# A decoder trunk on one core: the first eight expert picks multiplied one by one beside the retention of the second tile

## The chip, the cores and the metric

The kernel runs on one core of one Trainium2 chip. The metric is the device time of one execution in microseconds (us), and the smaller it is the better. Two numbers are used. The time of a run is what the device reports. The span is what the profiler sees from the first to the last instruction of one profiled execution.

The engines are PE (matmuls; PEld is its weight load), DVE (vector), ACT (activation functions and copies), POOL (here it issues the gathers) and SP (it issues the plain loads). All transfers run on the same 16 DMA engines.

## What is computed

256 tokens, in two tiles of 128, pass two layers of width 1024. Layer 0 mixes the tokens with a sparse attention and a retention, layer 1 with a convolution module. After each mixer stands the expert layer, which takes nearly all the bytes:

```python
def peer_ffn(h, w_q, sub_keys, u, v):
    q = (xf @ w_q).reshape(T, P_HEADS, 2, P_QDIM // 2)
    s1 = jnp.einsum('thd,kd->thk', q[:, :, 0], sub_keys[0])
    s2 = jnp.einsum('thd,kd->thk', q[:, :, 1], sub_keys[1])
    ...
    # top 16 of each, top 16 of their sums: 8 heads x 16 = 128 experts per token, with gates
    def block(args):
        xb, ib, gb = args
        hb = jnp.einsum('td,tkd->tk', xb, u[ib])
        act = jax.nn.gelu(hb, approximate=False) * gb
        return jnp.einsum('tk,tkd->td', act, v[ib])
```

Each token picks 128 experts of 16384, and an expert is one row of u and one of v, 8 KB together in float32. A *pick* below is the k-th expert of all 128 tokens of a tile: one gather of 128 rows of 2048 floats, 1.049 MB. There are 128 picks for each of two tiles in each of two layers, 512 in all.

The retention of layer 0, which the change works beside, is for a tile and a head: q times k, times a decay, times v (and for the second tile also against the first tile's k and v), then a norm over the head, then a product with the swish of a gate. Then attention and retention go through one output projection w_o into the residual, which the expert layer reads.

## The kernel before

The program is written out by hand for five engines, each a queue of instructions in program order, with semaphores between them.

**The ring.** Expert rows are gathered into a ring of 16 slots of 1 MB in SBUF. For pick n, POOL issues the gather (line 498). DVE multiplies the u half with the token's normed input and sums it: one dot per token (line 1042). ACT makes the gelu of the dots of two picks (line 654), times the gates (line 657), and writes it as diagonal matrices of 64 columns (line 663). PE multiplies the v half with the diagonals (line 1491) into accumulators and counts `v_multiplied`. This count frees the slot for a later pick. A round is 16 picks, eight rounds are a tile, and PE, ACT and DVE have other work written in between the picks of a round (the functions `first_beside` and `beside`).

PE multiplies picks in pairs. The matrices are 64 x 64 quadrants of the array: an even pick uses the two quadrants on one diagonal and adds into the PSUM tile `side`, an odd pick those on the other diagonal and adds into `pm`.

**What POOL waits for before it issues pick n.** (a) The slot's last pick was multiplied. `pick_slots` gives each pick its slot and the pick that must be multiplied first. Up to pick 127 this is pick n - 14, because slots 14 and 15 are away, and hold weights, from pick 14 on (`AWAY`). (b) Pick n - 5 has landed (`AHEAD`). (c) The picks of the first round also wait for what lay in the ring before: the input weights w_in and the work tiles of attention and retention. Slots 0 to 2 are free when the second tile's attended values are copied out (`a_ready`), slots 3 to 6 after the projection rq of the second tile, 7 and 8 after its rv, 9 and 10 after its rg (the gate), and 11 and up when the retained values have been copied out (`b_t_ready`). (d) Each round needs its 16 indices, which DVE writes head by head (`heads`, lines 950 to 1028); POOL copies them first (line 481).

**The place of the change** is the end of the second tile's mixer, from 126 to 164 us. PE goes through this order: queries for head 1, attended values, scores, then the projections rq and rv, retention scores, the retained product, the projection rg, the transposes of the result, and after that picks 0, 1, 2, ... ACT and DVE are written in the same order. Among picks 0 to 15 PE also multiplies the queries and scores of heads 2 and 3, with the weight chunks 2 and 3 of wq. SP loads these into slots 14 and 15, and waits for `b_t_ready` of the second tile before it does (`load_kept`, line 387). Once the scores are there, DVE does the selection for both heads in one piece, `heads(0, 1)` at line 1216, after the dots of pick 15 and before the dots of pick 16.

Of the kernel before, what the change touches and what calls it, by code (L numbers as in the profile page):

```python
# [7 lines left out]
D = 1024  # L8
# [29 lines left out]
AHEAD = 5  # L38
BATCH = 4
HALF = P // 2  # L40
COLS = D // 2
# [19 lines left out]
KEPT_IN = {(kind, p, c): r for kind, p, c, r in KEPT}  # L61
AWAY = {10: (PICKS + 6 * RING, 3 * PICKS + RING + 4), 11: (PICKS + 6 * RING, 3 * PICKS + RING + 4), 12: (PICKS, 2 * PICKS + 2 * RING + 12), 13: (PICKS, 2 * PICKS + 2 * RING + 12), 14: (RING - 2, 3 * PICKS + 2 * RING + 8), 15: (RING - 2, 3 * PICKS + 2 * RING + 8)}

# [27 lines left out]
def pick_slots():  # L91

    last, uses, slots = {r: r - RING for r in range(RING)}, {r: 0 for r in range(RING)}, []
    for n in range(4 * PICKS):
        free = [r for r in range(RING) if r not in AWAY or not AWAY[r][0] <= n < AWAY[r][1]]
        r = min(free, key=lambda r: last[r])
        uses[r] += 1
        slots.append((r, uses[r], max(last[r], n - RING)))
        last[r] = n
    return slots  # L100
# [20 lines left out]
def hybrid_decoder_trunk_kernel(nc, x, gains, w_in, kv_norm, uk_t, uv_w, w_o, rot, decay,  # L121
# [9 lines left out]
    with ctx:  # L131
# [314 lines left out]
        def _(pool):  # L446
# [24 lines left out]
            def gathers(p, first, end):  # L471

                layer, t = p // 2, p % 2
                for i in range(first, end):
# [6 lines left out]
                    pool.tensor_copy(idx_now[:, i % 2, :], eidx[:, t, i * RING:(i + 1) * RING]).then_inc(idx_copied, 1)  # L481
                    pool.wait_ge(idx_copied, n0 // RING + 1)
                    for n in range(n0, n0 + RING):
                        r, use, freed = SLOTS[n]
                        if freed >= 0:
                            pool.wait_ge(v_multiplied, RING + freed + 1)
                        if n < RING and r in in_use:
                            if in_use[r]:
                                pool.wait_ge(proj_ps, job_of(*in_use[r]) + 1)
                            else:  # L490
                                pool.wait_ge(b_t_ready, 2)
                        if r in AWAY and n >= AWAY[r][1] and all(SLOTS[m][0] != r for m in range(AWAY[r][1], n)):
                            kind, of, c = [k[:3] for k in KEPT if k[3] == r][-1]
                            pool.wait_ge(*((pw_ps, KD + c + 1) if kind == "w1" else (q_ps, nth_head(of + 1, c // 2, c % 2))))
                        if n >= AHEAD:
                            pool.wait_ge(gathered[SLOTS[n - AHEAD][0]], 16 * SLOTS[n - AHEAD][1])
                        pool.sem_inc(may_gather, 1)
                        pool.indirect_dma_start(ring[:, r, :], None, table[layer],  # L498
                                                bass.IndirectOffsetOnAxis(idx_now[:, i % 2, n - n0:n - n0 + 1], 0)) \
                            .then_inc(gathered[r], 16)  # L500

            pool.wait_ge(a_ready, 2)
            gathers(0, 0, 8)
# [8 lines left out]
        def _(act):  # L512
# [134 lines left out]

            def expert_round(p, i, between=None):

                t = p % 2  # L650
                for first, end in batches(p, i):
                    n0 = p * PICKS + i * RING
                    act.wait_ge(dots_ready, n0 + end)
# [95 lines left out]
            gate_exps(0, 0, (1,))  # L749
            keep_rv(1)  # L750
            root_of_group_norm(1)
            gate_of_retention(1)
            keep_retained(1)
            for i in range(8):
                expert_round(0, i, lambda b: first_beside(i, b))
                if i == 0:
                    gate_exps(0, 1)
            for p in (1, 2, 3):
# [16 lines left out]
        def _(dve):  # L775
# [255 lines left out]

            def expert_round(p, i, between=None):


                t = p % 2

                for r in range(RING):
                    if between:
# [115 lines left out]
            heads(0, 0, (1,))  # L1154
            rotary(1, 0)
            decay_scores(1)
            group_norm(1)
# [56 lines left out]

            expert_round(0, 0)
            heads(0, 1)
# [10 lines left out]
        def _(pe):  # L1227
# [220 lines left out]

            def queries(p, i, b):
# [4 lines left out]
                for j in range(2):  # L1454
                    last = product(ps_q[:, b, j * P:(j + 1) * P], lambda k: w[:, k, j * P:(j + 1) * P], lambda k: of_tile[:, k, :])
                last.then_inc(q_ps, 1)
# [17 lines left out]

            def expert_round(p, i, between=None):

                if p and i == 0:
                    pe.wait_ge(x_ready, (0, 3, 5, 7)[p])
                last_pick = (RING - 1, RING - 3) if (p, i) == LAST else (RING - 2, RING - 1)
                for first, end in batches(p, i):  # L1480
                    for r0 in range(first, end, 2):
                        pair = range(r0, min(r0 + 2, end))
                        pe.wait_ge(diag_ready, p * PICKS + i * RING + pair[-1] + 1)
                        for c in range(2):
                            for r in pair:
                                odd = r % 2 if (p, i) != LAST or r < RING - 1 else 0
                                for half in range(2):
                                    rows = slice(half * HALF, (half + 1) * HALF)
                                    j = (half + odd) % 2
                                    slot = SLOTS[p * PICKS + i * RING + r][0]  # L1490
                                    step = pe.matmul(acc[odd][c][j * HALF:(j + 1) * HALF, :], diag[rows, r % (2 * BATCH), :],  # L1491
                                                     ring[rows, slot, D + c * COLS:D + (c + 1) * COLS],
                                                     start=(i == 0 and r0 == 0), stop=(i == 7 and r == last_pick[odd]))
                                if c and ((p, i) != LAST or r < RING - 1):
                                    step.then_inc(v_multiplied, 1)
                                elif (p, i) == LAST and r == RING - 1:
                                    step.then_inc(last_ps, 1)
                    if between and end % BATCH == 0:
# [96 lines left out]

            for i in range(8):
                expert_round(0, i, lambda b: first_beside(i, b))
# [70 lines left out]
```

## Time and profile before

| | us |
|---|---|
| median of 3 runs | 1567.49 |
| lowest and highest of them | 1563.81, 1574.69 |
| the profiled execution's own time | 1567.84 |
| its span | 1566.1 |
| DMA engines, bytes moved | 611.75 MB, mean 391 GB/s |
| PE, DVE, ACT, POOL busy | 68%, 70%, 33%, 45% of the span |

The page cuts the span into 40 equal slices of 39 us each. Slices 2 to 4 (39 to 157 us) are those in which the DMA engines are less than busy; from slice 5 on they are at 9 tenths or more throughout, at 380 to 422 GB/s up to the last slice. The first gather is issued at 133.4 us.

### The profile page before, as it was taken

The page shows a single profiled execution, that of the slowest core. Times are in us where ns is not written, and L with a number is a line of the kernel's source. Part 1 is how long each engine was busy: PE and PEld are TensorE (multiplying, and loading weights), DVE is VectorE, ACT ScalarE, POOL GpSimd, SP SyncE. Part 2 cuts the span into 40 slices and gives each one's busy share as a digit, 9 for nine tenths or more (in the row PEclk, how much of TensorE's full clock was granted, in tenths as well). Part 3 has the DMA queues.
Part 4 walks back from the last instruction along what each step waited for, and adds up shares of the span by engine and source line. Part 5 has one row for each costly group of instructions (what it writes and reads, how often), then busy time and mean ns, then how long its engine had stood idle before and what let it go on. Part 6 is the DMA issues. An engine that isn't in the chain of part 4 may idle for free.

```text
span 1566.1 us, 20662 instructions
## 1 busy us (share of the span) xinstructions
PE 1057.7 (68%) x6966; PEld 528.1 (34%) x6966; DVE 1101.3 (70%) x2839; ACT 514.7 (33%) x1569; POOL 710.1 (45%) x566
## 2 busy tenths in 40 slices
PE   7999857666674576667746678646767657565655
PEld 7796433332331143323413335312433313111111
DVE  2745567787887678986448889899558878654455
ACT  3222314333232444324313443434243234322223
POOL 0002434344444366675334436575444445454552
PEclk9999978888787788887768889967887879778686
DMA  9147999999999999999999999999999999999996
GB/s 381 55 145 269 372 421 421 420 420 421 418 413 420 416 389 422 416 392 422 421 421 396 406 380 421 420 422 417 420 421 421 420 418 418 410 422 421 421 421 272
DMA packets 85451, 611.75 MB, mean 391 GB/s; under 512 B 9440, under 2 KB 10208, under 8 KB 12640
## 3 DMA queue, kind: packets, MB, share of 16 engines
q0 software_dynamic: 73728, 536.90, 83.2%
q1 hardware_dynamic: 11472, 73.26, 11.6%
q8 instruction: 55, 0.90, 0.2%
q14 instruction: 52, 0.43, 0.1%
q10 hardware_dynamic: 144, 0.26, 0.0%
HBM read 609.34 MB, written 1.05 MB: 390 GB/s over the span
## 4 chain that ended last, share of the span: by engine, by line
DMA 76%; PE 13%; DVE 7%; ACT 2%; issue 1%; DVEq 1%; ACTq 0%; POOL 0%; SPq 0%; POOLq 0%
DMA ring<-experts_dram,idx_now 75%; PE pm L1239 6%; PE side L1491 3%; DVE ring L1042 2%; PE side L1239 2%; DMA ring<-wq_dram 1%; DMA x_tok<-x_dram 0%; PE pm L1380 0%; ACT diag_all L663 0%; PE side L1462 0%; DVE top_i L962 0%; DVE x_tok L1056 0%; DVE onehot L963 0%; DVE top_i L978 0%; DVE conv_buf L1111 0%
## 5 line engine op out<-in xcount | busy, mean ns | idle before, releaser
L498 POOL DMA_INDIRECT ring<-experts_dram,idx_now x512 | 692.5, 1353 | 708.8 <-DMA ring<-experts_dram,idx_now 421.2
L1491 PE MATMUL side<-ring,diag_all 64*64 64x512 f32 x2056 | 650.8, 772 | 476.6 <-ACT diag_all L663 468.0
L1042 DVE SCALAR_TENSOR_TENSOR ring<-ring,h_tok 128x1024 f32<-128x1024 f32 x512 | 611.1, 1224 | 249.5 <-DMA ring<-experts_dram,idx_now 242.7
L1491 PE MATMUL pm<-ring,diag_all 64*64 64x512 f32 x2040 | 647.5, 773 | 0.0
L1491 PEld LDWEIGHTS side<-ring,diag_all 64*64 64x64 f32 x2056 | 153.1, 162 | 897.4 <-ACT diag_all L663 646.6
L654 ACT ACTIVATE ge<-hb 128x2 f32<-128x2 f32 (+1 forms) x257 | 52.4, 204 | 830.7 <-DVE ring L1042 830.3
L663 ACT ACTIVATE diag_all<-ident,act_v 128x64 f32<-128x64 f32 x512 | 150.7, 341 | 21.3 <-issue 0.4
L1491 PEld LDWEIGHTS pm<-ring,diag_all 64*64 64x64 f32 x2040 | 151.7, 162 | 0.0
L657 ACT ACTIVATE act_v<-ge,gates 128x1 f32<-128x1 f32 x512 | 123.5, 288 | 17.7
L1111 DVE SCALAR_TENSOR_TENSOR conv_buf<-conv_buf,chan_sb 128x128 f32<-128x128 f32 x480 | 128.9, 348 | 0.0
L1239 PEld LDWEIGHTS side<-h_t,wbuf 128*128 128x128 f32 x448 | 52.3, 195 | 13.3 <-issue 10.6
L1239 PE MATMUL side<-h_t,wbuf 128*128 128x128 f32 x448 | 54.6, 281 | 2.2 <-ACT h_t L526 2.2
L1239 PE MATMUL pm<-conv_buf,ring 128*128 128x128 f32 x448 | 53.6, 280 | 0.2 <-DVE ring L889 0.2
L654 ACT ACT_TABLE_LOAD x41 | 52.6, 1283 | 1.6
L1239 PEld LDWEIGHTS pm<-conv_buf,ring 128*128 128x128 f32 x448 | 52.3, 194 | 1.4 <-DVE ring L889 0.6
L959 DVE MAX8 top_v<-side 128x8 f32<-128x128 f32 x64 | 15.2, 290 | 49.8 <-PE side L1462 49.6
L481 POOL COPY idx_now<-eidx 128x16 uint32<-128x16 uint32 x32 | 11.0, 345 | 73.1 <-ACT conv_buf L605 72.9
L1042 DVE DVE_READ_ACCUMULATOR ring<-ring,h_tok 128x1 f32 x512 | 42.7, 83 | 0.0
L1239 PEld LDWEIGHTS side<-h_t,ring 128*128 128x128 f32 x320 | 38.6, 201 | 10.5 <-issue 7.3
L1239 PE MATMUL side<-h_t,ring 128*128 128x128 f32 x320 | 40.3, 287 | 2.2 <-DMA ring<-wq_dram 2.2
L1239 PEld LDWEIGHTS pm<-hc_t,wbuf 128*128 128x128 f32 x256 | 32.1, 207 | 10.0 <-issue 10.0
L1239 PE MATMUL pm<-wbuf,hc_t 128*128 128x256 f32 x128 | 32.0, 414 | 5.1 <-DMA wbuf<-w_dram 5.1
(207 smaller groups left out, 967.4 us busy)
## 6 DMA issues: line engine op xcount, KB each, us to landing
wbuf<-wq_dram SPq DMA_DIRECT2D x16, 1024.0 KB, 9.2
wbuf<-w_dram SPq DMA_DIRECT2D x16, 1024.0 KB, 9.7
ring<-w_in_dram SPq DMA_DIRECT2D x5, 2048.0 KB, 22.5
wbuf<-w_o_dram SPq DMA_DIRECT2D x8, 1024.0 KB, 5.3
ring<-experts_dram,idx_now POOLq DMA_INDIRECT x512, 11.6
ring<-wq_dram SPq DMA_DIRECT2D x6, 1024.0 KB, 11.9
ring<-w_dram SPq DMA_DIRECT2D x4, 1024.0 KB, 9.2
gain<-gains_dram SPq DMA_DIRECT2D x7, 512.0 KB, 12.6
```

The costliest lines, as they stand in the source:

```text
L481: pool.tensor_copy(idx_now[:, i % 2, :], eidx[:, t, i * RING:(i + 1) * RING]).then_inc(idx_copied, 1)
L498: pool.indirect_dma_start(ring[:, r, :], None, table[layer], bass.IndirectOffsetOnAxis(idx_now[:, i % 2, n - n0:n - n0 + 1], 0)) \
L654: act.activation(ge[:, first:end], hb[:, first:end], ACT.Gelu)
L657: last = act.activation(act_v[:, r:r + 1], ge[:, r:r + 1], ACT.Copy, scale=gates[:, t, i * RING + r:i * RING + r + 1])
L663: act.activation(diag[:, r % (2 * BATCH), :], ident2[:, :], ACT.Copy, scale=act_v[:, r:r + 1]).then_inc(diag_ready, 1)
L959: dve.max(top_v[:, b, j, 0:8], side[b, j])
L1042: dve.scalar_tensor_tensor(out=ring[:, slot, 0:D], in0=ring[:, slot, 0:D], scalar=1.0, in1=h_tok[:, t, :], op0=ALU.mult, op1=ALU.mult, acc ...
L1111: step = dve.scalar_tensor_tensor(out=dst, in0=src, scalar=tap, in1=dst, op0=ALU.mult, op1=ALU.add)
L1239: last = pe.matmul(dst, lhs(k), rhs(k), start=(k == 0), stop=(k == KD - 1))
L1491: step = pe.matmul(acc[odd][c][j * HALF:(j + 1) * HALF, :], diag[rows, r % (2 * BATCH), :], ring[rows, slot, D + c * COLS:D + (c + 1) * COLS],
```

## The change

PE, ACT and DVE are written in another order around the end of the second tile's mixer. The projection rg comes directly after rv. Picks 0 to 7 are multiplied one at a time (`SINGLES = 8`), each into the even accumulator `side` only, since `pm` still holds the retention: four before the retention scores, two between these and the retained product, two behind it. Slots 14 and 15 are not given to picks of the first round, and slots 11 to 13 not before pick 19 (`LATE`); picks 11 to 18 take slots 0 to 7 again. On POOL the wait for `a_ready` stands behind the copy of the indices, and on PE the attended values stand in the middle of the queries of head 1. Behind the retention, PE multiplies picks 8 to 11, then both queries of heads 2 and 3, then picks 12 to 15, then scores and output products.

```diff
+SINGLES = 8
+LATE = {11: 19, 12: 19, 13: 19}
...
-AWAY = {..., 14: (RING - 2, 3 * PICKS + 2 * RING + 8), 15: (RING - 2, 3 * PICKS + 2 * RING + 8)}
+AWAY = {..., 14: (0, 3 * PICKS + 2 * RING + 8), 15: (0, 3 * PICKS + 2 * RING + 8)}
...
-        free = [r for r in range(RING) if r not in AWAY or not AWAY[r][0] <= n < AWAY[r][1]]
+        free = [r for r in range(RING) if n >= LATE.get(r, 0) and (r not in AWAY or not AWAY[r][0] <= n < AWAY[r][1])]
...
                     pool.wait_ge(idx_copied, n0 // RING + 1)
+                    if n0 == 0:
+                        pool.wait_ge(a_ready, 2)
...
-                        if n < RING and r in in_use:
+                        if use == 1 and r in in_use:
...
-            pool.wait_ge(a_ready, 2)
             gathers(0, 0, 8)
...
             keep_rv(1)
+            expert_round(0, 0, part=(0, BATCH))
+            gate_of_retention(1)
+            expert_round(0, 0, part=(BATCH, SINGLES))
             root_of_group_norm(1)
-            gate_of_retention(1)
             keep_retained(1)
-            for i in range(8):
+            expert_round(0, 0, part=(SINGLES, SINGLES + BATCH))
+            first_beside(0, 1)
+            expert_round(0, 0, part=(SINGLES + BATCH, RING))
+            first_beside(0, 2)
+            gate_exps(0, 1)
+            for i in range(1, 8):
...
             rotary(1, 0)
+            expert_round(0, 0, part=(0, SINGLES))
             decay_scores(1)
...
-            expert_round(0, 0)
+            expert_round(0, 0, part=(SINGLES, RING))
             heads(0, 1)
...
-            def expert_round(p, i, between=None):
+            def multiply(p, i, picks):
+
+                pe.wait_ge(diag_ready, p * PICKS + i * RING + picks[-1] + 1)
...
+                first_pick = (0, 1) if p else (0, SINGLES + 1)
+                for c in range(2):
+                    for r in picks:
+                        alone = (p, i) == LAST and r == RING - 1 or (p, i) == (0, 0) and r < SINGLES
+                        odd = 0 if alone else r % 2
...
-            queries(0, 0, 1)
-            attended_values(1)
+            queries(0, 0, 1, lambda: attended_values(1))
             scores(0, 0, 1)
             pe.wait_ge(a_ready, 2)
             project("rq", 1)
             project("rv", 1)
+            project("rg", 1)
+            for r in range(BATCH):
+                multiply(0, 0, (r,))
             retention_scores(1)
+            for r in range(BATCH, BATCH + 2):
+                multiply(0, 0, (r,))
             retain(1)
-            project("rg", 1)
+            for r in range(BATCH + 2, SINGLES):
+                multiply(0, 0, (r,))
             transpose_retained(1)
...
-            for i in range(8):
+            expert_round(0, 0, part=(SINGLES, SINGLES + BATCH))
+            first_beside(0, 0)
+            first_beside(0, 1)
+            expert_round(0, 0, part=(SINGLES + BATCH, RING))
+            first_beside(0, 2)
+            first_beside(0, 3)
+            for i in range(1, 8):
```

**PE, from the queries of head 1 to picks 0 and 1, before.** L1239 is any product over eight chunks (queries into `side` from `wbuf`; rq into `pm` from `conv_buf`; rv and rg into `pm` from `ring`), L1388 the attended values, L1462 the scores, L1312 the retention scores, L1324 and L1326 the retained product (eight rows, of which two stand here), L1332 the transposes of it, L1491 the picks.

```order
L1239 MATMUL side<-h_t,wbuf 128x128 x16
L1388 MATMUL pm<-ring 64x128 x8
L1462 MATMUL side<-keys_sb,q_t 128x128 x2
L1239 MATMUL pm<-conv_buf,ring 128x128 x32
L1239 MATMUL pm<-ring,conv_buf 128x512 x8
L1312 MATMUL pm<-ring 128x128 x16
L1324 MATMUL pm<-ring 128x128
L1326 MATMUL pm<-ring 128x128
...
L1239 MATMUL pm<-ring,conv_buf 128x512 x8
L1332 MATMUL pm<-ident,ring 128x128 x4
L1491 MATMUL side<-ring,diag_all 64x512 x2
L1491 MATMUL pm<-ring,diag_all 64x512 x2
```

The same place with the change (line numbers are those of the changed kernel, 10 to 12 higher; L1500 are the picks):

```order
L1249 MATMUL side<-h_t,wbuf 128x128 x8
L1398 MATMUL pm<-ring 64x128 x8
L1249 MATMUL side<-h_t,wbuf 128x128 x8
L1474 MATMUL side<-keys_sb,q_t 128x128 x2
L1249 MATMUL pm<-conv_buf,ring 128x128 x32
L1249 MATMUL pm<-ring,conv_buf 128x512 x16
L1500 MATMUL side<-ring,diag_all 64x512 x16
L1322 MATMUL pm<-ring 128x128 x16
L1500 MATMUL side<-ring,diag_all 64x512 x8
L1334 MATMUL pm<-ring 128x128
...
L1500 MATMUL side<-ring,diag_all 64x512 x8
L1342 MATMUL pm<-ident,ring 128x128 x4
```

The projection rg now stands before the retention scores, and 32 matmuls of single picks stand between it and the transposes: four picks (16 rows), two, and two.

**POOL, picks 10 to 15, before**, each row an issue with the semaphores it waits for (`gathered` is the landing of pick n - 5, `v_multiplied` a slot that must have been multiplied):

```order
L498 DMA ring<-experts0_dram,idx_now 128x2048 [waits gathered5]
L498 DMA ring<-experts0_dram,idx_now 128x2048 [waits b_t_ready,gathered6]
L498 DMA ring<-experts0_dram,idx_now 128x2048 [waits gathered7]
L498 DMA ring<-experts0_dram,idx_now 128x2048 [waits gathered8]
L498 DMA ring<-experts0_dram,idx_now 128x2048 [waits v_multiplied,gathered9]
L498 DMA ring<-experts0_dram,idx_now 128x2048 [waits v_multiplied,gathered10]
```

With the change, picks 10 to 15, and after the lines left out picks 18 and 19:

```order
L502 DMA ring<-experts0_dram,idx_now 128x2048 [waits gathered5]
L502 DMA ring<-experts0_dram,idx_now 128x2048 [waits v_multiplied,gathered6]
L502 DMA ring<-experts0_dram,idx_now 128x2048 [waits v_multiplied,gathered7]
L502 DMA ring<-experts0_dram,idx_now 128x2048 [waits v_multiplied,gathered8]
L502 DMA ring<-experts0_dram,idx_now 128x2048 [waits v_multiplied,gathered9]
L502 DMA ring<-experts0_dram,idx_now 128x2048 [waits v_multiplied,gathered10]
...
L502 DMA ring<-experts0_dram,idx_now 128x2048 [waits v_multiplied,gathered2]
L502 DMA ring<-experts0_dram,idx_now 128x2048 [waits gathered3,v_multiplied,b_t_ready]
```

The wait for `b_t_ready` has moved from pick 11 to pick 19, and picks 11 to 18 wait for picks 0 to 7 to be multiplied.

## Rows read from the trace of the kernel before

**Rows 1.** The page: span, busy share of the 16 DMA engines in 40 slices, chain

```profile
span 1566.1 us, 20662 instructions
...
DMA  9147999999999999999999999999999999999996
...
DMA 76%; PE 13%; DVE 7%; ACT 2%; issue 1%; DVEq 1%; ACTq 0%; POOL 0%; SPq 0%; POOLq 0%
```

**Rows 2.** Windows: stretch, us, busy time of PE, PEld, DVE, ACT, POOL; PEclk, DMA, GB/s

```profile
...
132.00:158.00 26.00, 24.64 (x140) 17.79 (x140) 14.60 (x54) 3.81 (x7) 8.89 (x10) 1.00 0.96 381
158.00:164.00 6.00, 3.09 (x10) 1.18 (x8) 2.81 (x5) 1.25 (x3) 1.88 (x2) 0.95 0.38 117
158.00:159.00 1.00, 1.00 (x4) 0.39 (x3) 0.00 (x0) 0.00 (x0) 0.00 (x0) 1.00 0.84 352
162.00:163.00 1.00, 0.37 (x3) 0.37 (x4) 1.00 (x2) 0.00 (x0) 0.69 (x2) 1.00 0.27 49
164.00:180.00 16.00, 11.69 (x88) 6.11 (x92) 12.47 (x22) 8.44 (x31) 9.38 (x7) 0.81 1.00 417
180.00:230.00 50.00, 32.66 (x228) 18.52 (x220) 31.78 (x97) 11.56 (x39) 19.49 (x19) 0.83 1.01 421
```

**Rows 3.** Timeline of POOL, 132 to 223 us: start, us, engine, line, op [idle <-releaser]

```profile
132.24 0.20 POOL L481 COPY idx_now<-eidx 128x16 uint32<-128x16 uint32 x1 [72.89 <-ACT conv_buf L605]
...
133.39 1.15 POOL L498 DMA_INDIRECT ring<-experts_dram,idx_now  x1 [0.96 <-POOL idx_now L481]
...
147.61 0.94 POOL L498 DMA_INDIRECT ring<-experts_dram,idx_now  x1 [2.23 <-PE pm L1239]
...
149.08 0.94 POOL L498 DMA_INDIRECT ring<-experts_dram,idx_now  x1 [0.54 <-issue]
...
161.27 0.94 POOL L498 DMA_INDIRECT ring<-experts_dram,idx_now  x1 [11.25 <-PE pm L1239]
...
222.13 1.65 POOL L498 DMA_INDIRECT ring<-experts_dram,idx_now  x1 [2.94 <-DMA ring<-experts_dram,idx_now]
```

**Rows 4.** Timeline of PE, 146 to 222 us

```profile
146.70 3.50 PE L1312 MATMUL pm<-ring 64*128 64x128 f32 x32
...
153.40 7.03 PE L1239 MATMUL pm<-ring,conv_buf 128*128 128x512 f32 x16
...
173.68 3.84 PE L1239 MATMUL side<-h_t,ring 128*128 128x128 f32 x32 [1.61 <-DMA ring<-wq_dram]
...
196.10 0.71 PE L1462 MATMUL side<-keys_sb,q_t 128*128 128x128 f32 x4
...
217.61 1.12 PE L1491 MATMUL side<-ring,diag_all 64*64 64x512 f32 x2 [17.34 <-ACT diag_all L663]
...
221.07 0.75 PE L1491 MATMUL side<-ring,diag_all 64*64 64x512 f32 x2
```

**Rows 5.** Timeline of ACT, 130 to 164 us

```profile
130.43 0.37 ACT L636 COPY q_t<-side 128x256 f32<-128x256 f32 x1 [2.56 <-PE side L1239]
...
131.46 0.59 ACT L605 COPY conv_buf<-pm 128x512 f32<-128x512 f32 x1 [0.66 <-PE pm L1388]
...
163.32 0.59 ACT L585 COPY conv_buf<-pm 128x512 f32<-128x512 f32 x1 [2.25 <-PE pm L1332]
```

**Rows 6.** Timeline of DVE, 155 to 178 us

```profile
155.57 1.37 DVE L870 TENSOR_SCALAR ring<-pm,rstd_y 128x128 f32<-128x128 f32 x4
...
161.10 0.69 DVE L821 TENSOR_TENSOR ring<-pm,ring 128x512 f32<-128x512 f32 x1 [4.16 <-ACT ring L576]
...
177.70 1.23 DVE L1042 SCALAR_TENSOR_TENSOR ring<-ring,h_tok 128x1024 f32<-128x1024 f32 x1 [2.46 <-DMA ring<-experts_dram,idx_now]
```

**Rows 7.** Timeline of all engines at the end: two picks multiplied one by one

```profile
1556.19 3.60 PE L1491 MATMUL side<-ring,diag_all 64*64 64x512 f32 x16
```

**Rows 8.** Line 498 (gathers), then tile wq_dram (weight chunks): issue to landing

```profile
...
DMA to landing us min/median/max: 5.7/11.6/19.1
...
DMA to landing us min/median/max: 4.6/9.7/18.2
```

More of the change, by code:

```diff
@@ L61 @@
 KEPT_IN = {(kind, p, c): r for kind, p, c, r in KEPT}
-AWAY = {10: (PICKS + 6 * RING, 3 * PICKS + RING + 4), 11: (PICKS + 6 * RING, 3 * PICKS + RING + 4), 12: (PICKS, 2 * PICKS + 2 * RING + 12), 13: (PICKS, 2 * PICKS + 2 * RING + 12), 14: (RING - 2, 3 * PICKS + 2 * RING + 8), 15: (RING - 2, 3 * PICKS + 2 * RING + 8)}
+AWAY = {10: (PICKS + 6 * RING, 3 * PICKS + RING + 4), 11: (PICKS + 6 * RING, 3 * PICKS + RING + 4), 12: (PICKS, 2 * PICKS + 2 * RING + 12), 13: (PICKS, 2 * PICKS + 2 * RING + 12), 14: (0, 3 * PICKS + 2 * RING + 8), 15: (0, 3 * PICKS + 2 * RING + 8)}
 def kept_as(kind, p, c):
@@ L646, in gate_exps, with expert_round @@
                     act.activation(expo[:, b, :], lead[:, b, :], ACT.Exp, accum_out=expo_sum[:, b:b + 1]).then_inc(gate_exp, 1)
-            def expert_round(p, i, between=None):
+            def expert_round(p, i, between=None, part=(0, RING)):
                 t = p % 2
                 for first, end in batches(p, i):
+                    if not part[0] <= first < part[1]:
+                        continue
                     n0 = p * PICKS + i * RING
@@ L750, in _ @@
             keep_rv(1)
+            expert_round(0, 0, part=(0, BATCH))
+            gate_of_retention(1)
+            expert_round(0, 0, part=(BATCH, SINGLES))
             root_of_group_norm(1)
-            gate_of_retention(1)
             keep_retained(1)
-            for i in range(8):
+            expert_round(0, 0, part=(SINGLES, SINGLES + BATCH))
[4 more added lines that the diff above has]
+            for i in range(1, 8):
                 expert_round(0, i, lambda b: first_beside(i, b))
-                if i == 0:
-                    gate_exps(0, 1)
             for p in (1, 2, 3):
@@ L1030, in put_picks, with expert_round @@
                 dve.drain()
-            def expert_round(p, i, between=None):
+            def expert_round(p, i, between=None, part=(0, RING)):
                 t = p % 2
-                for r in range(RING):
+                for r in range(*part):
                     if between:
@@ L1447, in heads_start, with queries @@
                     pe.wait_ge(small_loaded, 32)
-            def queries(p, i, b):
+            def queries(p, i, b, halfway=None):
                 w = chunk("q", 0 if p == 1 and i >= 2 else p, 2 * i + b)
@@ L1454, in queries @@
                 for j in range(2):
+                    if j and halfway:
+                        halfway()
                     last = product(ps_q[:, b, j * P:(j + 1) * P], lambda k: w[:, k, j * P:(j + 1) * P], lambda k: of_tile[:, k, :])
@@ L1473, in both_scores @@
                     scores(p, i, b)
-            def expert_round(p, i, between=None):
+            def multiply(p, i, picks):
+                pe.wait_ge(diag_ready, p * PICKS + i * RING + picks[-1] + 1)
+                last_pick = (RING - 1, RING - 3) if (p, i) == LAST else (RING - 2, RING - 1)
+                first_pick = (0, 1) if p else (0, SINGLES + 1)
[3 more added lines that the diff above has]
+                        odd = 0 if alone else r % 2
+                        slot = SLOTS[p * PICKS + i * RING + r][0]
+                        for half in range(2):
+                            rows = slice(half * HALF, (half + 1) * HALF)
+                            j = (half + odd) % 2
+                            step = pe.matmul(acc[odd][c][j * HALF:(j + 1) * HALF, :], diag[rows, r % (2 * BATCH), :],
+                                             ring[rows, slot, D + c * COLS:D + (c + 1) * COLS],
+                                             start=(i == 0 and r == first_pick[odd]), stop=(i == 7 and r == last_pick[odd]))
+                        if c and ((p, i) != LAST or r < RING - 1):
+                            step.then_inc(v_multiplied, 1)
+                        elif (p, i) == LAST and r == RING - 1:
+                            step.then_inc(last_ps, 1)
@@ L1477, in expert_round @@
+            def expert_round(p, i, between=None, part=(0, RING)):
                 if p and i == 0:
                     pe.wait_ge(x_ready, (0, 3, 5, 7)[p])
-                last_pick = (RING - 1, RING - 3) if (p, i) == LAST else (RING - 2, RING - 1)
                 for first, end in batches(p, i):
[L1481 to L1497, printed above, removed]
@@ L1498, in expert_round @@
+                    if not part[0] <= first < part[1]:
+                        continue
+                    multiply(p, i, range(first, end))
                     if between and end % BATCH == 0:
```

## The prediction

> **What bounds the kernel now.** I read the page first. The chain that ended last is three quarters DMA, and the 16 DMA engines are at 9 tenths from the fifth slice to the end [rows 1]. From 164 us on a window moves 417 to 421 GB/s at a share of 1.00 or more [rows 2], and a pick of 1.049 MB takes 2.49 us at 421. So the time is the bytes over that rate, plus every stretch in which the DMA engines starve after the first gather. An edit is worth only the starving that it takes away or adds. Shorter work on PE, DVE or ACT is worth nothing by itself.
>
> Then the windows around the change. Between 158 and 164 us the DMA engines move 117 GB/s instead of 421 [rows 2], so 6 x (1 - 117/421) = 4.3 us are lost. POOL's timeline says why: pick 8 is issued at 149.08, pick 9 only at 161.27, after 11.25 us of waiting for PE [rows 3], which is the projection rg from 153.40 to 160.43 [rows 4].
>
> **Part 1, the start of the gathers.** POOL copied the indices at 132.24 and issued the first gather at 133.39 [rows 3]. Now the copy is done earlier, and the issue follows the attended values' copy at once. These were out at 131.46 + 0.59 = 132.05 [rows 5]. Setting them between the two halves of the queries doesn't bring them out earlier: ACT's queue has the copy of the queries (130.43, [rows 5]) ahead of the copy of the attended values, and the queries now end 1.0 us later, since the attended product stands inside them. 130.43 + 1.0, 0.3 to the next copy and 0.59 give 132.3. So the first gather goes out at about 132.5, 0.9 earlier, and rq, which waits for the same signal, starts 0.2 later. I book 0.8.
>
> **Part 2, the hole.** rg (7.03, [rows 4]) now follows rv, and ends at 146.7 + 0.2 + 7.0 = 153.9. POOL saw the end of rv 0.8 after it (146.8 to 147.61, [rows 3, 4]), so pick 9 goes out at 154.7, before the flow of pick 8 ends (158.8, below; 157.9 with the earlier start). Picks 11 to 18 wait for picks 0 to 7. A pick multiplied alone costs half of 3.60 = 1.8 us [rows 7], so four end at 161.1, the retention scores (3.5, [rows 4]) at 164.6, picks 4 and 5 at 168.2, the retained product, for which I take 2.0 of the 3.2 between the scores' end and rg [rows 4], at 170.2, picks 6 and 7 at 173.8. With 0.8 for POOL, picks 11 to 14 are issued from 156.5 to 161.9, 15 and 16 at 167 and 169, 17 and 18 at 173 and 174.6. The DMA engines need pick 11 at about 163, and one every 2.49 us after it, pick 18 at 180. Each issue is at least 5 us early, and all 4.3 us of the hole go. With part 1 the stream of picks is **5.1 us** ahead.
>
> **Part 3, what becomes late.** The retained values come out later. DVE needs 3.5 us from the product's end through the norm (153.4 to 156.94) and 1.5 for swish and gate (161.10 to 162.57) [rows 4, 6], and transposes and copy need 1.3 more, to 163.91 [rows 5]: 170.2 + 6.3 = 176.5, which is 12.6 later. Pick 19 waits for that, and is in time. SP also waits for it before it loads the two wq chunks. Before, PE started on the first at 173.68, after waiting for it [rows 4], 9.7 us after the signal; now at 186.2. DVE is free at 175.2 and takes picks 8 to 11 at 1.2 each [rows 6], so PE has multiplied them by about 183.5. Then, at the lengths of before, both queries end at 193.6 (3.7 each), picks 12 to 15 at 197.0 (3.46 for two at half clock, so 0.86 for one at the full), and after one score (0.6) and one output product (3.6, as it has half the columns of rg) the scores of the last head start at 201.2, where they started at 196.10 [rows 4]. That is **S = 5.1 us later** for the selection of both heads on DVE and for the dot of pick 16, which stands behind it.
>
> Pick 30 needs pick 16's slot (30 - 14). PE multiplied picks 16 and 17 from 217.61 to 221.07 after 17.34 us of idleness, at half clock [rows 4]; now until 226.2, and pick 30 is issued at 227.0. Before it was issued at 222.13, released by a landing [rows 3], so the stream, 5.1 us ahead, wants it at 217.0. It is 10.0 us late. How long do the engines live on what is in flight? From the issue at 149.08 the flow held to about 158.8 (352 of 421 in that window, [rows 2]), 9.7 us; the median gather needs 11.6 us to land [rows 8]. Off these come 2.5 us, after which the next issue is normal, and 1.4 from an issue to its flow (161.27 to about 162.7, [rows 2, 3]). The cushion is 5.8 to 7.7 us. The new hole is 2.3 to 4.2 us; I take the middle, 3.3, as neither row is nearer.
>
> **The sum.** -0.8 - 4.3 + 3.3 = **-1.8 us** (-2.8 to -0.9). Once pick 30 waits, the 5.1 us cancel: the net is S - 0.1 - cushion. The twice as long singles (8 x 0.9 = 7.2 us more of PE) and two more table loads on ACT are inside these times, or wait beside the chunk's landing, with 2.7 us to spare. Their cover gone, they would count one for one. Picks 132 to 137 get 12 slots instead of 14, and picks 227 to 231 get 10 or 11 instead of 12. The kernel before goes over to 12 slots at pick 138 and to 10 at pick 232 itself, with the DMA slices there at 9 tenths [rows 1], so I book nothing. From 1567.84 of the profiled execution this gives 1566.0. The median stands 0.35 under that execution; I say 1566.
>
> **A rule against the trace.** The chunk's 9.7 us were measured when POOL had just resumed; now five gathers stand in flight. The rows of all such chunks spread from 4.6 to 18.2 us, median 9.7 [rows 8].
> The Trainium skill ("DMA: Bandwidth & Descriptors", section "Queues, rings and completion order") says that each DMA engine takes turns between queues, packet by packet, so that a chunk on SP's queue doesn't stand behind POOL's backlog. By it the sum stays as above; were the order that of issue, the chunk would come some 8 us later, which is the second rival. The chunk row's median agrees with the rule, its maximum doesn't.
>
> **Rivals.**
> - *Nothing is given back.* The cushion is longer than I think, or S under 2.7 us, and pick 30 finds the engines fed. Then -5.1: 1562.7. For it: the share is 1.01 from 180 to 230 us, through the 17 us in which PE waits for the selection [rows 2]. Against it: there, pick 30 was just in time. 0.22.
> - *The chunk comes late, the other sign.* With the longest landing, 18.2 instead of 9.7, S is 13.6 and the net 13.6 - 0.1 - 6.8 = +6.7: 1574.5. It costs from S = 6.8 on, a landing 1.7 us over mine. 0.20.
> - *PE at the low level.* In the windows PE runs at 1.00, the 2.4 GHz level, while busy [rows 2]. Should waits for diagonals drop it to 1.2 GHz between 153.9 and 176.5, its 20 us there double: S = 25, net +18: 1586. 0.04.
> - *A later stage starves on the shallower ring*, or shrinks, by more than a slice's worth. 0.03 to either side.
>
> My forecast has the rest, 0.48.
>
> **The numbers.** Seven tenths of the chance lie between 1562 and 1568. The runs shown spread from 1563.8 to 1574.7 about their median, so I add some 3 us: **1559 to 1576**, leaving out the half-clock case and the tails. One per cent, 15.7 us, is about what a measurement of this kernel tells from no change. Faster by more needs over three times the hole: 0.03. Slower by more: the half-clock case and some of the shallow ring, 0.06. Within: 0.91.
>
> **What would show it.** The window 158 to 164 at full rate, and pick 9 issued near 154.7. The first gather near 132.5. The copy of the retained values near 176.5, the queries after a wait for the chunk near 186, picks 16 and 17 multiplied by about 226. A window near 225 below 421 GB/s, with POOL waiting for PE at pick 30, is the give-back; none there means the first rival. A granted clock of 0.5 between 154 and 176 is the third. If the DMA engines starve between 160 and 180, the order of the singles is wrong in my account, and so is the sum.

## The result: about 4 us slower, not 2 us faster

The changed kernel takes 1572.03 us (median of 22 runs, 1566.96 to 1574.37). The kernel before took 1568.73 us in as many runs beside it. The ratio on record is 1.0026, with a 95% interval of 1.0018 to 1.0035: 4.1 us slower (2.8 to 5.5); it isn't the quotient of the two medians, which stand 3.3 us apart. Gains and losses below are worked out from such ratios. The forecast was 1.8 us faster. The time lies inside the range that was given and within 1%, but the sign is wrong, and the whole interval lies on the other side of zero.

### The profile after

The page answers to [rows 1]:

```profile
span 1569.7 us, 20668 instructions
...
DMA  9146979999999999999999999999999999999996
...
DMA 76%; PE 14%; DVE 6%; issue 2%; ACT 1%; DVEq 1%; ACTq 0%; SPq 0%; another core or an unknown queue 0%; POOLq 0%; POOL 0%
```

Two digits of the DMA row are new. The sixth slice (196 to 235 us) stands at 7 where it stood at 9. The fourth (118 to 157 us) stands at 6 where it stood at 7, but up to 158 us the two kernels have moved the same bytes within 0.1 MB (33.9 before, 33.8 with the change), so only the sixth counts. Windows (the columns are those of [rows 2]) find the place:

```profile
132.00:158.00 26.00, 26.00 (x121) 15.16 (x121) 19.05 (x54) 9.18 (x23) 12.15 (x12) 1.00 0.99 384
158.00:164.00 6.00, 6.00 (x48) 3.91 (x44) 1.24 (x2) 2.55 (x6) 2.84 (x3) 1.00 1.01 418
164.00:200.00 36.00, 27.98 (x189) 15.52 (x189) 15.02 (x34) 9.06 (x26) 12.53 (x13) 0.91 1.01 421
200.00:222.00 22.00, 6.79 (x34) 5.70 (x32) 17.45 (x72) 1.79 (x5) 3.75 (x4) 0.73 0.98 409
222.00:231.00 9.00, 6.95 (x40) 3.10 (x41) 8.56 (x16) 5.08 (x20) 2.32 (x2) 0.71 0.07 21
```

The hole of before is closed: 158 to 164 us moves 418 GB/s instead of 117. A larger one has opened 60 us later. Between 222 and 231 us the DMA engines move 21 GB/s, so 9 x (1 - 21/421) = 8.6 us are lost there. The last two windows in the kernel before:

```profile
200.00:222.00 22.00, 4.66 (x26) 1.43 (x28) 21.02 (x65) 5.47 (x20) 6.60 (x6) 0.61 1.02 422
222.00:231.00 9.00, 9.00 (x63) 4.88 (x56) 2.54 (x5) 1.42 (x6) 5.64 (x6) 1.00 1.01 421
```

POOL's timeline of the changed kernel, which answers to [rows 3]; the rows are the index copy, the first gather, pick 9, and picks 29 and 30:

```profile
127.14 0.20 POOL L483 COPY idx_now<-eidx 128x16 uint32<-128x16 uint32 x1 [68.28 <-DVE eidx L1038]
132.97 1.14 POOL L502 DMA_INDIRECT ring<-experts_dram,idx_now  x1 [5.63 <-ACT conv_buf L608]
...
154.45 1.69 POOL L502 DMA_INDIRECT ring<-experts_dram,idx_now  x1 [3.29 <-DMA ring<-experts_dram,idx_now]
...
209.51 0.94 POOL L502 DMA_INDIRECT ring<-experts_dram,idx_now  x1 [2.48 <-issue]
228.38 1.84 POOL L502 DMA_INDIRECT ring<-experts_dram,idx_now  x1 [17.93 <-PE pm L1500]
```

For 18 us POOL waits for PE to have multiplied pick 16, and issues nothing. PE's timeline, which answers to [rows 4]:

```profile
153.55 7.08 PE L1500 MATMUL side<-ring,diag_all 64*64 64x512 f32 x32
160.56 3.50 PE L1322 MATMUL pm<-ring 64*128 64x128 f32 x32
163.99 3.65 PE L1500 MATMUL side<-ring,diag_all 64*64 64x512 f32 x16
...
174.71 0.66 PE L1342 MATMUL pm<-ident,ring 128*128 128x128 f32 x4 [1.51 <-DVE ring L885]
...
185.10 3.84 PE L1249 MATMUL side<-h_t,ring 128*128 128x128 f32 x32 [0.68 <-DMA ring<-wq_dram]
191.37 3.84 PE L1249 MATMUL side<-h_t,ring 128*128 128x128 f32 x32 [2.42 <-DMA ring<-wq_dram]
...
202.73 0.61 PE L1474 MATMUL side<-keys_sb,q_t 128*128 128x128 f32 x4
...
224.05 1.12 PE L1500 MATMUL side<-ring,diag_all 64*64 64x512 f32 x2 [17.26 <-ACT diag_all L668]
...
227.37 0.59 PE L1500 MATMUL side<-ring,diag_all 64*64 64x512 f32 x2
```

The scores of the last head are at 202.73 (before 196.10), pick 16 starts at 224.05 (before 217.61), and the row at 227.37 is the first of picks 18 and 19, so picks 16 and 17 are done then. PE idles for 17.3 us in both kernels, while DVE makes the selection of heads 2 and 3 in one piece. SP's two weight chunks go out at 176.02 (ACT's copy of the retained values is done at 175.99):

```profile
176.02 0.80 SPq L393 DMA_DIRECT2D ring<-wq_dram  x2
202.93 4.23 SPq L404 DMA_DIRECT2D wbuf<-w_o_dram  x2
```

Over 164 to 264 us the changed kernel moves 379 GB/s and so loses about 10 us, where the kernel before lost almost nothing. Taking off the 4.3 of the closed hole and the 0.4 by which the first gather is earlier leaves 5.3 for this pair of traces. Some 1.9 us of it come back later: the kernel before moves 418 GB/s from 300 to 500 us and 407 from 500 to 700, the changed one 420 and 409. From 960 to 1300 both move 420.

### The profile page after: what moved, and what is told of

It is laid out like the page before. It is cut to its first block, busy times and chain, and to the rows that moved or that the text cites. A ratio compares the mean times of both kernels' runs of the same rounds, so it can differ in the third digit from the quotient of the medians.

```text
span 1569.7 us, 20668 instructions
## 1 busy us (share of the span) xinstructions
PE 1070.2 (68%) x6966; PEld 531.4 (34%) x6966; DVE 1100.9 (70%) x2839; ACT 516.5 (33%) x1571; POOL 690.9 (44%) x566
## 3 DMA queue, kind: packets, MB, share of 16 engines
q1 hardware_dynamic: 11472, 73.26, 11.6%
## 4 chain that ended last, share of the span: by engine, by line
DMA 76%; PE 14%; DVE 6%; issue 2%; ACT 1%; DVEq 1%; ACTq 0%; SPq 0%; another core or an unknown queue 0%; POOLq 0%; POOL 0%
DMA ring<-experts_dram,idx_now 74%; PE pm L1249 6%; PE side L1500 3%; DVE ring L1051 2%; PE side L1249 2%; DMA ring<-wq_dram 2%; DMA x_tok<-x_dram 0%; PE side L1474 0%; PE pm L1390 0%; DVE x_tok L1065 0%; DVE top_i L972 0%; DVE onehot L973 0%; DVE top_i L988 0%; ACT diag_all L668 0%; DVE diag_all L1000 0%
## 5 line engine op out<-in xcount | busy, mean ns | idle before, releaser
L502 POOL DMA_INDIRECT ring<-experts_dram,idx_now x512 | 672.4, 1313 | 736.8 <-DMA ring<-experts_dram,idx_now 464.2
L1500 PE MATMUL side<-ring,diag_all 64*64 64x512 f32 x2088 | 664.1, 776 | 467.2 <-ACT diag_all L668 457.5
L1500 PE MATMUL pm<-ring,diag_all 64*64 64x512 f32 x2008 | 645.9, 783 | 0.0
L1500 PEld LDWEIGHTS side<-ring,diag_all 64*64 64x64 f32 x2088 | 156.8, 163 | 897.6 <-ACT diag_all L668 635.1
L1500 PEld LDWEIGHTS pm<-ring,diag_all 64*64 64x64 f32 x2008 | 151.5, 164 | 0.0
L1249 PEld LDWEIGHTS side<-h_t,wbuf 128*128 128x128 f32 x448 | 53.2, 198 | 13.5 <-issue 10.7
L969 DVE MAX8 top_v<-side 128x8 f32<-128x128 f32 x64 | 15.3, 288 | 59.3 <-PE side L1474 58.2
## 6 DMA issues: line engine op xcount, KB each, us to landing
ring<-experts_dram,idx_now POOLq DMA_INDIRECT x512, 11.6
```

The lines of the kernel that those rows point to most:

```text
L502: pool.indirect_dma_start(ring[:, r, :], None, table[layer], bass.IndirectOffsetOnAxis(idx_now[:, i % 2, n - n0:n - n0 + 1], 0)) \
L969: dve.max(top_v[:, b, j, 0:8], side[b, j])
L1249: last = pe.matmul(dst, lhs(k), rhs(k), start=(k == 0), stop=(k == KD - 1))
```

## The experiments

Eight kernels, each timed in five rounds (11 or 12 executions each, but only 5 each for the two with the chunks loaded later). Ratios are to the kernel before on the same chip, and a ratio of 1.001 is 1.57 us. That kernel's median beside them was 1567.69 for the two reorderings of the dots, the early chunks and the early copy, and 1567.33 for the other four.

### Pick 16 multiplied before the selection, in the changed kernel

If the hole at pick 30 is what costs, taking pick 16 off the selection must bring the whole gain. DVE takes the dots of picks 16 to 19 before `heads(0, 1)`, and ACT makes their diagonals before the exponentials.

```diff
+EARLY = 4
...
             first_beside(0, 2)
+            expert_round(0, 1, lambda b: first_beside(1, b), part=(0, EARLY))
             gate_exps(0, 1)
-            for i in range(1, 8):
+            expert_round(0, 1, lambda b: first_beside(1, b), part=(EARLY, RING))
+            for i in range(2, 8):
...
             expert_round(0, 0, part=(SINGLES, RING))
+            expert_round(0, 1, part=(0, EARLY))
             heads(0, 1)
```

> The changed kernel, and in it DVE and ACT take picks 16 to 19 before the selection of heads 2 and 3 and not behind it (PE's order is as it was). Theory A (the changed kernel loses at pick 30, which waits for the slot of pick 16, and pick 16 waits behind the selection): picks 30 to 33 find their slots by about 211 us, the hole of 220 to 230 us (9.9 us) closes but for 1 us or less, and the stream keeps the 5.1 us that it gained before. Against the kernel before 0.997 (1564, from 1563 to 1566), against the change 9 us less. Theory B (the loss is made later, by the shallower ring from pick 132 on or the other places of the chunk loads): the hole may close, but the time stays within 2 us of the changed kernel, 1570 to 1573.

Measured: 1562.27 us, ratio 0.9960 (0.9946 to 0.9973), 4.2 to 8.5 us faster than the kernel before. The windows of its trace:

```profile
158.00:164.00 6.00, 6.00 (x46) 3.92 (x42) 0.66 (x2) 2.56 (x6) 2.57 (x4) 1.00 1.00 416
164.00:200.00 36.00, 27.94 (x188) 15.43 (x188) 19.70 (x42) 11.41 (x36) 15.05 (x14) 0.91 1.01 421
200.00:222.00 22.00, 12.20 (x71) 8.36 (x70) 17.45 (x73) 1.79 (x5) 6.18 (x7) 0.81 1.01 421
222.00:231.00 9.00, 9.00 (x53) 5.42 (x53) 4.47 (x9) 2.55 (x10) 4.22 (x4) 0.89 1.01 421
```

Pick 30 goes out at 209.65. The chunks and the scores are as late as in the changed kernel (queries at 185.29 and 191.50, scores at 202.87), yet no window starves. The closed hole and the earlier start are worth 4.3 + 0.4 = 4.7 us, which the interval takes in (its middle is 6.3), and up to 264 us this trace has moved 5.2 us of full flow more than the kernel before. So the lateness of the chunks costs only through pick 16, and the shallower ring of the later rounds costs nothing that shows here. This kernel is faster than both.

### The same reordering alone, in the kernel before

The same edit without the singles. It tells whether the early dots are worth something by themselves.

```diff
+            expert_round(0, 0, lambda b: first_beside(0, b))
+            expert_round(0, 1, lambda b: first_beside(1, b), part=(0, EARLY))
+            gate_exps(0, 1)
...
             expert_round(0, 0)
+            expert_round(0, 1, part=(0, EARLY))
             heads(0, 1)
```

> The kernel before with the same edit: picks 16 to 19 before the selection. There was no hole at pick 30 in the kernel before, so theory A expects nothing: 1568.7, within 1.5 us. If the early dots were a gain of their own (theory C: the selection's place costs time elsewhere too), it is 1566 or less.

Measured: 1568.36 us, ratio 1.0006 (0.9992 to 1.0020), no difference. Pick 30 is issued at 219.87 instead of 222.13, and nothing comes of it, as nothing was lost there before:

```profile
217.40 0.94 POOL L499 DMA_INDIRECT ring<-experts_dram,idx_now  x1 [1.17 <-DMA ring<-experts_dram,idx_now]
219.87 1.97 POOL L499 DMA_INDIRECT ring<-experts_dram,idx_now  x1 [1.54 <-DMA ring<-experts_dram,idx_now]
```

With pick 16 out of the way, pick 30 follows pick 29 after the usual 2.47 us. The hole from 158 to 164 us stays (142 GB/s). The change alone loses, the early dots alone give nothing that shows, and the two together gain.

### The two weight chunks loaded earlier, in the changed kernel

Chunk 2 goes as soon as the retention scores are out of the work tiles, chunk 3 when the product's operand is free; the slots are swapped for it.

```diff
-KEPT = [("q", 0, 2, 14), ("q", 0, 3, 15), ...
+KEPT = [("q", 0, 2, 15), ("q", 0, 3, 14), ...
...
-                    sp.wait_ge(b_t_ready, 2)
+                    sp.wait_ge(*((ret_s_ready, 2) if r == 15 else (b_ready, 2)))
```

> The changed kernel, and SP loads the two kept chunks of wq earlier: the first into slot 15 as soon as the second tile's decayed scores are written (about 165 us, was 176.0), the second into slot 14 once the gated product is (174.7). Theory A: both queries run right after picks 8 to 11, the scores of the last head start near 199.4 instead of 202.7, and the hole of 9.9 us shrinks by those 3.3 us: 1.0005 of the kernel before (1569.5, 1568 to 1571). If the chunks' landing is not in the chain of that hole, the time stays at that of the change.

Measured: 1567.50 us, ratio 0.9998 (0.9986 to 1.0011). POOL around pick 30, and the window:

```profile
209.03 0.94 POOL L502 DMA_INDIRECT ring<-experts_dram,idx_now  x1 [3.92 <-issue]
224.94 1.87 POOL L502 DMA_INDIRECT ring<-experts_dram,idx_now  x1 [14.97 <-PE pm L1500]
```

```profile
222.00:231.00 9.00, 9.00 (x60) 4.55 (x56) 5.57 (x11) 3.34 (x14) 4.61 (x5) 0.90 0.39 128
```

PE waits for no chunk now, and pick 30 goes 3.4 us earlier than in the changed kernel. Against that kernel's ratio 4.4 us are gained, which the intervals do not tell from the 3.4. The hole shrinks and doesn't close, and the kernel is level with the one before.

### Both edits

The early dots and the early chunks, in the changed kernel.

> The changed kernel with both edits: picks 16 to 19 before the selection, and the kept chunks loaded earlier. With the early dots alone no hole was left between 200 and 240 us (420 to 422 GB/s in each window), so there is nothing for the earlier chunks to give: 0.996 of the kernel before, 1562 to 1563, within 1.5 us of the early dots alone. If theory A missed a second wait on these chunks, it is 3 us less.

Measured: 1564.19 us, ratio 0.9976 (0.9966 to 0.9986), so 1.9 us above the early dots alone and a little above the 1562 to 1563 expected. The windows from 158 to 240 us are full, as with the early dots alone. Once pick 16 is off the selection, no gain from the earlier chunks shows. The interval overlaps that of the early dots alone; whether the small difference between them is real stays open.

### The indices copied first, in the kernel before

```diff
                     pool.wait_ge(idx_copied, n0 // RING + 1)
+                    if n0 == 0:
+                        pool.wait_ge(a_ready, 2)
...
-            pool.wait_ge(a_ready, 2)
             gathers(0, 0, 8)
```

> The kernel before with one part of the change alone: POOL copies the indices before it waits for the attended values. The first gather goes out at about 132.5 instead of 133.4. Whether this counts depends on picks 3 and 9, which wait for projections: the stream starves from 159 to 163 us all the same, and the 0.9 us are lost there again. Expected 0.0 us, at most 0.9 less.

Measured: 1567.34 us, ratio 0.9998 (0.9985 to 1.0011): no gain that can be told. In its trace the work up to the first gather lies some 3 us earlier as a whole, so only differences within it are read. Its pick 30 answers a question that [rows 3] left open:

```profile
213.32 1.88 POOL L500 DMA_INDIRECT ring<-experts_dram,idx_now  x1 [1.54 <-issue]
219.28 1.65 POOL L500 DMA_INDIRECT ring<-experts_dram,idx_now  x1 [4.08 <-PE pm L1492]
```

In a kernel that is the one before from here on, pick 30 is released by PE. PE's pick 16:

```profile
214.76 1.12 PE L1492 MATMUL side<-ring,diag_all 64*64 64x512 f32 x2 [17.36 <-ACT diag_all L664]
```

The issue follows 4.52 us after this start. In the kernel before the two stand 4.52 apart as well (217.61 and 222.13), though the row names a landing as the releaser. In the five other traces in which pick 30 is held up, it is 4.3 to 4.5.

### The gate product alone moved, in the kernel before

rg directly after rv, no singles, the old slots.

```diff
             keep_rv(1)
-            root_of_group_norm(1)
             gate_of_retention(1)
+            root_of_group_norm(1)
...
             project("rv", 1)
+            project("rg", 1)
             retention_scores(1)
             retain(1)
-            project("rg", 1)
```

> The kernel before with one part of the change alone: the projection rg directly behind rv, on PE and ACT. Picks in pairs, slots, and the order of all else are as before. Picks 9 and 10 go out at about 154.5 instead of 161.3, but the retention now comes behind rg and its result about 3 us later (167), and picks 11 on and the chunks wait for it. The hole of 4.3 us shrinks to between 0 and 2 us (two picks last 5 us, from 159 to 164, and pick 11 comes at 168), and the selection comes 3 us later, which takes about the 2 to 3 us in hand at pick 30. Together 1566 to 1569, at most 2.5 us less than before.

Measured: 1568.50 us, ratio 1.0006 (0.9995 to 1.0017). POOL, picks 10 and 11:

```profile
152.74 0.94 POOL L498 DMA_INDIRECT ring<-experts_dram,idx_now  x1 [0.30 <-issue]
165.00 1.62 POOL L498 DMA_INDIRECT ring<-experts_dram,idx_now  x1 [11.32 <-ACT conv_buf L585]
```

The wait has moved from pick 9 to pick 11, which needs the retained values, and is as long as it was (11.3 us). The 238 GB/s of its window 158 to 164, the 403 of 164 to 200 and the 367 of 222 to 231 lose 2.6 + 1.5 + 1.2 = 5.3 us. So the gate product's place alone gains nothing; it takes the singles too, since they free slots for picks 11 to 18. The singles without the moved gate product were not run.

### The chunks loaded later, in both kernels

The loads wait for picks to have been multiplied: 4 in the kernel before, and 10 in the changed one.

```diff
-                    sp.wait_ge(b_t_ready, 2)
+                    sp.wait_ge(v_multiplied, RING + 4)
```

> The kernel before, with one wait made longer: SP loads the two kept chunks of wq once picks 0 to 3 are multiplied (about 171.9 us) and not at 163.9, so 8 us later; nothing else is changed. It measures how long the engines live on what is in flight at pick 30, the cushion that the prediction took as 5.8 to 7.7 us. The queries of heads 2 and 3 and what follows come 7 to 8 us later, pick 30 is issued near 229 and not 222.1. By the prediction's cushion the DMA engines starve for 0 to 2 us: 1568 to 1570. If pick 30 had only about 2 us in hand in the kernel before, they starve for some 5 us: 1573 to 1574.

Measured: 1576.33 us, ratio 1.0050 (1.0036 to 1.0064), so 7.8 us (5.6 to 10.0). Its POOL and its windows:

```profile
216.89 0.94 POOL L498 DMA_INDIRECT ring<-experts_dram,idx_now  x1 [1.85 <-issue]
233.37 1.65 POOL L498 DMA_INDIRECT ring<-experts_dram,idx_now  x1 [15.54 <-PE pm L1491]
```

```profile
222.00:231.00 9.00, 2.16 (x12) 0.80 (x16) 8.75 (x21) 2.46 (x10) 0.00 (x0) 0.50 0.81 333
231.00:240.00 9.00, 9.00 (x52) 4.46 (x48) 4.78 (x9) 2.62 (x11) 4.69 (x5) 0.81 0.47 158
```

The loss is larger than either figure expected, as the loads went out at 174.34, 10.4 us later and not 8, and pick 30 came 11.2 us later. The hole at pick 30 is there, made in the kernel before by the late chunks alone. A smaller one comes before it: PE's picks 4 and up stand behind the first chunk, POOL's pick 18 waits for pick 4 until 191.54, and 164 to 200 us moves 387 GB/s instead of 419. In the changed kernel (`RING + 10`):

> The changed kernel, with the kept chunks loaded once picks 8 and 9 are multiplied (about 182.2 us) and not at 176.0: 6 us later. Theory A: the changed kernel already starves at pick 30, so each us by which the selection comes later is a us of the whole: 1.0065 of the kernel before, 6 us more than the change (1578 to 1580). If the hole of the changed kernel had another cause than the lateness of the chunks, it grows by less than 2 us.

Measured: 1578.73 us, ratio 1.0069 (1.0055 to 1.0082), 10.8 us slower than the kernel before (8.6 to 12.9), 6.7 more than the change, as expected. Pick 30 goes at 233.28.

### What the engines had in hand before pick 30

If pick 30 is tied to PE in every one of these, the loss should be its delay less one constant. The delay is counted from the first gather, since that shifts from run to run (88.74 us in the kernel before); for the last three rows 0.4 is taken off for the earlier start.

| kernel | first gather | pick 30 | later by | measured, us | in hand |
|---|---|---|---|---|---|
| before, chunks late | 133.06 | 233.37 | 11.6 | +7.8 (5.6 to 10.0) | 3.8 (1.6 to 6.0) |
| changed | 132.97 | 228.38 | 6.3 | +4.1 (2.8 to 5.5) | 2.2 (0.8 to 3.5) |
| changed, chunks early | 133.01 | 224.94 | 2.8 | -0.3 (-2.2 to 1.7) | 3.1 (1.1 to 5.0) |
| changed, chunks late | 130.67 | 233.28 | 13.5 | +10.8 (8.6 to 12.9) | 2.7 (0.6 to 4.9) |

All four allow 1.6 to 3.5 us. Three of them exclude the 5.8 to 7.7 of the prediction, and the first only touches its lower end. The intervals are those of the times alone; pick 30 was read in one execution of each, which for the first row was the slowest of its five.

The traces tell more. Every kernel here has moved the same 22.8 MB by 110 us, so the bytes moved up to a later time (windows of 1 us added up) say how far a kernel is behind the one before, in us of full flow. At 264 us only the losses up to the hole are in it:

| kernel | pick 30, later than 222.13 by | behind at 264 us | in hand | behind at 700 us |
|---|---|---|---|---|
| before, chunks late | 11.2 | 10.4 | 0.8 | 8.8 |
| changed | 6.3 | 5.5 | 0.8 | 3.7 |
| changed, chunks early | 2.8 | 2.2 | 0.6 | 0.3 |
| changed, chunks late | 11.2 | 10.3 | 0.9 | 8.6 |
| before, gate product moved | -1.2 | -2.0 | 0.8 | -3.8 |

So at pick 30 only 0.6 to 0.9 us were in hand, in five traces out of five. Between 264 and 700 us these five then get 1.6 to 1.9 us back, most of it from 400 to 600 us; the four other kernels, which don't starve at pick 30, get 0.0 to 0.6. The two together, 2.4 to 2.6, lie within what the times allow. Why a kernel that starved at pick 30 loses less there is open.

## Why the prediction was wrong, point by point

**What bounds the kernel: right.** Every time here follows the stretches in which the DMA engines starve. (Of the slices said to stand at 380 GB/s or more before, the fifth moves 372.)

**Part 1, the start.** The first gather came at 132.97, for 132.5 forecast, 0.4 earlier instead of 0.9. The attended values' copy ended at 131.43 + 0.59 = 132.02, no earlier than before, as said, but the issue followed it by 0.95 us, for which 0.2 were taken. In the kernel before, the same edit alone gave nothing that can be measured.

**Part 2, the hole: right.** Pick 9 went at 154.45 (154.7), four singles took 7.08 and two 3.65, the window is full. With the early dots on top the gain comes out in the time (4.2 to 8.5 us), so it was real and was given back.

**Part 3, S** (by how much the scores of the last head start later). The retained values were out at 175.99 (176.5), the first chunk was in at 185.1 (186), but the second only at 191.4, 15.3 us after the common issue, for which the prediction allowed no wait. That was no bad luck. The landings of the same two loads in the kernel before (line 391, 163 to 165 us):

```profile
DMA to landing us min/median/max: 9.7/12.1/14.6
```

The second was in only 14.6 us after its issue there too, but PE had picks 4 to 7 to multiply between the two queries and began the second at 181.04. The change puts the queries directly behind each other, and the landing shows. S became 6.6 us instead of 5.1, and pick 30 went 1.4 us later than forecast (228.4 for 227.0). The Trainium skill ("DMA: Bandwidth & Descriptors", section "Queues, rings and completion order") has queues take turns; the first chunk's 9.1 us agree with it, and the second's 15.3 us lie within the spread of [rows 8], so these two times don't decide in which order the queues were served.

**The failed step: the cushion.** This is how late pick 30 can be issued before the DMA engines starve. The prediction took 5.8 to 7.7 us. By the bytes it was 0.6 to 0.9, and with what comes back later the times behave as if it were 1.6 to 3.5. With S as forecast and 2.5 for the cushion the sum would have been 5.0 - 2.5 = +2.5 us, so the step alone turns the sign, and the 1.4 of S bring it to 3.9, near the 4.1 measured. (With 0.8, 5.0 - 0.8 + 1.4 = 5.6 us, and the trace is 5.5 behind at 264 us.) Three sizes in it were wrong:

- *The issue of 222.13 was read as the moment at which the stream wanted pick 30*, because the row names a landing. It was PE: the interval of 4.52 us from pick 16's start is the same in the twin whose row names PE, and with the early dots in the kernel before pick 30 goes at 219.87. The issue before it (the row below) stands 4.80 us earlier, not the normal 2.49, so 2.3 us of the cushion were already used.
- *The life on what is in flight.* Up to 231 us the changed kernel moved 313 x 121 = 37.9 MB from 110 us on, all it had issued before pick 30. The kernel before had moved 323 x 112 = 36.2 MB by 222 us, with the same loads. The rest, 1.7 MB, lasts 4 us, so it would have run dry at 226, 8.7 us after the issue of pick 29, where 9.7 to 11.6 were taken. These sums are good to about half a microsecond.
- *From the issue to the flow* 1.4 us were taken, read from rows of before. After 228.38 the three windows from 230 to 233 below count as 1.3 us of full flow, so it starts at about 231.7 in effect, 3.3 us after the issue. That reading was short already: there 162 to 163 us moved 49 GB/s and 163 to 164 only 172, so with 393 from 164 to 165 the flow after the issue of 161.27 starts at about 163.5 in effect, 2.3 us later.

```profile
217.33 1.87 POOL L498 DMA_INDIRECT ring<-experts_dram,idx_now  x1 [1.55 <-issue]
...
163.00:164.00 1.00, 0.29 (x3) 0.05 (x1) 1.00 (x3) 0.66 (x2) 0.46 (x1) 0.68 0.84 172
...
230.00:231.00 1.00, 1.00 (x6) 0.89 (x5) 0.56 (x2) 0.79 (x4) 0.70 (x2) 1.00 0.23 33
231.00:232.00 1.00, 1.00 (x6) 0.88 (x5) 0.00 (x0) 0.00 (x0) 0.66 (x2) 1.00 0.66 131
232.00:233.00 1.00, 1.00 (x9) 0.62 (x11) 0.06 (x1) 0.00 (x0) 0.49 (x1) 1.00 0.91 377
```

The first two rows are of the kernel before, the last three of the changed one. This leaves 8.7 - 4.8 - 3.3 = 0.6 us in hand, in line with the 0.6 to 0.9 of the five traces and far from the 6.8 that was taken.

**The rivals.** "Nothing is given back" is out by the window at 222 to 231. The late chunk was rated with a price from S = 6.8 on. That threshold was the cushion again, and so too high: S was 6.6, and it cost. The first chunk came as forecast and the second did not, so this rival gave part of the loss (the 1.4 us of S), though not by a landing of 18.2 us. Half clock is out: TensorE was granted 1.00 (its 2.4 GHz level) from 132 to 176 us, through the singles. The shallower ring is out by the experiment with the early dots.

The view that would have told it before was there: 17 us without PE work, POOL's gap of 4.8 us in front of pick 30, and pick 16 done just ahead of its issue. They were read as "just in time" for one rival's odds and not put into the sum.

## What to carry to other kernels

Before a stream is moved ahead, look for the next issue that is already tied to a compute engine: there the lead ends, and beyond the little that is in hand every microsecond by which the change delays that engine is lost. The slack is found from the gap between two issues and the bytes still to be moved, not from the releaser that one row names; where an issue stands a constant time behind an engine's row in several runs, that engine releases it. The repair lies at that tie (here four dots ahead of a long selection), and in this kernel neither edit is worth anything without the other.

## What the runs showed of the hardware

Two 1 MB loads issued together on SP's queue at 176.02, beside five gathers in flight, were in 9.1 and 15.3 us later: the second behind the first by 6.3 us, two and a half times the 2.49 that its bytes need at 421 GB/s. In the kernel before, with two gathers in flight at their issue, the same two loads took 9.7 and 14.6 us. Restarting the dry engines of the changed kernel cost 3.3 us from the issue to the effective flow, and with the 1.0 us from the end of picks 16 and 17 (227.37) to the issue, 4.3 us lie between the last matmul of pick 17 and full flow.
